# ScalarE's order of bank and weight cast in the FFN gate phases, turned round in both kinds of FFN

## The reference

```python
# first block, two layers; x (latent) and ctx (context) are 256 tokens each
def half_ffn(t, m, j):
    h = modulate(rmsnorm(t, norm_g[l, j]), m[3 * j], m[3 * j + 1])
    return t + 0.5 * m[3 * j + 2] * swiglu(h, ffn_w_gate[l, j // 2], ffn_w_up[l, j // 2], ffn_w_down[l, j // 2])
...
# second block, two layers; x only
x = x + 0.5 * swiglu_2(rmsnorm_2(x, ffn1_norm[l]), ffn1_w_in[l], ffn1_w_out[l])
...
x = x + 0.5 * swiglu_2(rmsnorm_2(x, ffn2_norm[l]), ffn2_w_in[l], ffn2_w_out[l])
```

## Time and profile before

| | |
|---|---|
| median of 3 runs | 3185.64 us (3184.75 to 3185.68) |
| the profiled execution's own time | 3185.47 us |
| its span, first to last instruction | 3183.7 us |
| PE busy | 3154.0 us, 99% |
| VectorE busy | 2373.9 us, 75% |
| ScalarE busy | 1346.6 us, 42% |
| GpSimd busy | 635.0 us, 20% |
| mean granted TensorE clock | 0.998 |

### The profile page before, as it was taken

One profiled execution on the slowest core, in us unless ns is written; L12 is line 12 of the kernel. 1 busy time (PEld: TensorE's weight loads), 2 busy tenths in 40 slices (PEclk: granted clock), 3 DMA queues, 4 the chain that ended last, 5 costly groups with the idle time before them and its releaser, 6 DMA issues.

```text
span 3183.7 us, 46362 instructions
## 1 busy us (share of the span) xinstructions
PE 3154.0 (99%) x17108; PEld 2708.8 (85%) x17108; DVE 2373.9 (75%) x3075; ACT 1346.6 (42%) x1987; POOL 635.0 (20%) x524
## 2 busy tenths in 40 slices
PE   9999999999999999999999999999999999999999
PEld 5888888888888888888888889889888889889988
DVE  4877957868787735566778887885888896885887
ACT  3222233212232224443546455565645546565643
POOL 2212322202321121001323230100222231100122
PEclk9999999999999999999999999999999999999999
DMA  6655514646365432334665665454665765453665
GB/s 235 209 156 175 162 57 147 201 139 188 96 198 176 139 102 87 106 106 140 195 187 163 196 177 169 133 152 140 184 193 174 201 186 172 127 157 114 192 193 151
DMA packets 771388, 507.47 MB, mean 159 GB/s; under 512 B 15108, under 2 KB 720720, under 8 KB 771216
## 3 DMA queue, kind: packets, MB, share of 16 engines
q1 hardware_dynamic: 770048, 503.51, 53.8%
q0 software_dynamic: 368, 1.38, 0.1%
q10 hardware_dynamic: 800, 0.24, 0.0%
HBM read 504.01 MB, written 1.05 MB: 159 GB/s over the span
## 4 chain that ended last, share of the span: by engine, by line
PE 51%; DVE 6%; issue 2%; ACT 2%; POOL 0%; DVEq 0%; ACTq 0%; POOLq 0%
PE bank L688 17%; PE bank L686 9%; PE bank L690 4%; PE bank L692 4%; PE bank L691 4%; PE bank L705 3%; PE bank L707 3%; PE bank L706 3%; PE bank L685 2%; DVE wlo_all L1675 2%; PE bank L1190 1%; ACT whi_all L1256 1%; PE bank L1016 0%; DVE xn_two L1773 0%; PE bank L1162 0%
## 5 line engine op out<-in xcount | busy, mean ns | idle before, releaser
L1675 DVE TENSOR_TENSOR wlo_all<-raw,whi_all 128x1024 fp32r<-128x1024 f32 (+3 forms) x768 | 1008.5, 1316 | 424.5 <-ACT whi_all L1256 421.8
L1256 ACT CAST whi_all<-raw 128x1024 fp32r<-128x1024 f32 (+3 forms) x768 | 833.6, 1091 | 1024.5 <-PE bank L692 551.4
L690 PE MATMUL bank<-xn_two,whi_all 128*128 128x512 f32 (+1 forms) x1616 | 587.9, 364 | 1.0 <-DVE xn_two L1849 1.0
L692 PE MATMUL bank<-xn_two,wlo_all 128*128 128x512 f32 (+1 forms) x1616 | 582.9, 361 | 0.0
L691 PE MATMUL bank<-xn_two,whi_all 128*128 128x512 f32 (+1 forms) x1616 | 582.7, 361 | 0.0
L688 PE MATMUL bank<-xn_two,whi_all 128*128 128x512 f32 x1540 | 550.4, 397 | 0.0
L2331 POOL CAST h_two<-silu_g 128x256 f32 (+1 forms) x176 | 209.3, 1189 | 1322.6 <-DVE silu_g L1914 753.4
L686 PE MATMUL bank<-xn_two,wlo_all 128*128 128x256 f32 x1760 | 456.1, 279 | 0.0
L686 PEld LDWEIGHTS bank<-xn_two,wlo_all 128*128 128x128 f32 x1760 | 332.5, 189 | 18.9
L690 PEld LDWEIGHTS bank<-xn_two,whi_all 128*128 128x128 f32 x1616 | 306.6, 190 | 47.5 <-DVE xn_two L1849 1.8
L691 PEld LDWEIGHTS bank<-xn_two,whi_all 128*128 128x128 f32 x1616 | 306.7, 190 | 45.7
(11 more groups left out here) (337 smaller groups left out, 4868.0 us busy)
## 6 DMA issues: line engine op xcount, KB each, us to landing
raw<-in_ffn_w_in SPq DMA_DIRECT2D x176, 512.0 KB, 3.8
raw<-in_w_in SPq DMA_DIRECT2D x168, 512.0 KB, 3.8
ada_w<-in_ada_w SPq DMA_DIRECT2D x128, 512.0 KB, 4.1
raw<-in_ffn_w_gate SPq DMA_DIRECT2D x88, 512.0 KB, 3.9
raw<-in_ffn_w_up SPq DMA_DIRECT2D x88, 512.0 KB, 4.2
raw<-in_ffn_w_down SPq DMA_DIRECT2D x32, 768.0 KB, 5.3
raw<-in_ret_w_in SPq DMA_DIRECT2D x48, 512.0 KB, 3.9
raw<-in_ffn_w_out SPq DMA_DIRECT2D x32, 768.0 KB, 4.9
```

The costliest lines, as they stand in the source:

```text
L690: pe.matmul(o, whi[s][:, k, :], hi, start=(k == 0), stop=False)
L692: return pe.matmul(o, wlo[s][:, k, :], hi, start=False, stop=(k == ks - 1))
L1256: act.copy(whi[s][:, 0:ks, :], raw[s][:, 0:ks, :]).then_inc(hi_done[s], 1)
L1675: tt(wlo[s][:, 0:ks, :], raw[s][:, 0:ks, :], whi[s][:, 0:ks, :].bitcast(F32), ALU.subtract).then_inc(lo_done[s], 1)
```

## The change

One expression in ScalarE's part of `do_ffn`:

```diff
-                    stream(f"{a['tag']}gu{half}", gate, weights_first=a["norm"]["late"])
+                    stream(f"{a['tag']}gu{half}", gate, weights_first=not a["norm"]["late"])
```

## The result

The changed kernel takes 3271.28 us (median of 4 runs, 3270.25 to 3272.57) against 3185.28 us: a ratio of 1.027, 95% interval 1.0257 to 1.0282. The forecast was 3284 us with a range of 3246 to 3308. The profiled execution has a span of 3269.7 us, 86.0 us over that of before.

What follows compares the result with a forecast made beforehand. PE bounds the kernel, VectorE only 0.33 us a pair quicker; the change makes VectorE the bound in late FFNs. 90.7 + 1.5 - 0.3 + 6.8 = 98.7 us over 3185.47 gives 3284 us, range 3246 to 3308.

Steps and rivals of the forecast that it cites:

- The pair: Late gate phases: VectorE's loop of two slots with ScalarE takes 6.76 us, against 5.26 before and PE's 5.59.
- R10: b01gu0, last round: start of VectorE's even reduce, counted from R0, the first; forecast at 2332.07.
- silu to split: Late gate phases: step of the pair with the cast in between, 1.39 us, taken from a11.
- The lead: Late gate phases: VectorE's lead is gone by pair 3 in gu0; PE waits from about pair 6 in gu1.
- L1885 term: b00gu0: eight L1885 in VectorE's queue, about 0.39 us each, four giving back 0.40 us each: +1.5 us.
- The multiply: Late FFNs: L1896's 0.83 us is half waiting on GpSimd and stays 0.83; were it free, the pair would be 6.36.
- Table loads: ScalarE: late gu0s lose 20, other FFNs gain 24, 1.28 us each; they cost nothing.
- The last product: Late dn phases: PE waits for GpSimd's last subtract, 2.6 us in dn0 and 3.2 us in dn1.
- The clock: Half-clock stretches after PE's eight waits for the last product: four taken, between 0 and 8, +6.8 us.
- The other four FFNs: a11's 0.29 us PE wait can go, wide FFNs' second table load is hidden: -0.3 us for all.
- No change: Rival: three slots of lead absorb the delay, decided by a pair at or below 5.59 us; 3185 us, chance 0.06.
- half clock for whole phases: Rival: clock falls for whole gate phases, a pair takes 11.2 us; 380 us more, 3566 us, chance 0.03.

Runs made afterwards that it cites:

- e3: e1, but in late FFNs VectorE splits the even slot behind the odd slot's product instead of ahead of its reduce; 3184.59 us (0.9998).
- e4: e1, but late FFNs leave out the multiply L1896, so the silu waits for the reduce; 3205.59 us (1.0065).
- e7: Changed kernel, but in late FFNs GpSimd's subtract (all but a phase's last) waits for VectorE's multiply L1896 of the next pair; 3246.15 us (1.0192).
- e2: Kernel before, but the other four FFNs (a00, a01, a10, a11) cast first, then bank; late FFNs as before; 3182.76 us (0.9995).
- e8: Changed kernel plus filler matmuls on PE between each late gu0 and its dn0 (eight asked, 16 in the trace); 3269.66 us (1.0268).
- e5: Changed kernel, but in late FFNs only gu0 takes the bank first, gu1 casts first as before; 3237.77 us (1.0165).
- e1: Kernel before, but only the four late FFNs take the bank first, then cast; the other four as before; 3273.52 us (1.0277).
- e6: Changed kernel, but in late FFNs only gu1 takes the bank first, gu0 casts first as before; 3216.68 us (1.0101).

## Why the prediction was right, and where it was off

**What bounds.** Right. PE had next to no wait to give back (1.2 us in the other four FFNs), VectorE had 0.33 us a pair to spare, and this is where the change struck.

**The pair.** Forecast 6.76, measured 6.78 and 6.85 in turn, every step within 0.07 us: the second kind has 1.50 instead of 1.43 us ahead of the split, as a11 before had 1.51 and 1.42. Of the 0.65 us by which b01gu0 exceeds the forecast, 0.5 us come so: the reduce R10 stands at 2332.58 where 2332.07 was forecast (2352.68 in the trace, less the 20.10). The rest is 0.07 us ahead of the last split, 0.02 us in it and 0.05 us from its end to dn0. e3 shows that the loss is VectorE's place behind the cast, and e4 and e7 that a step that gets shorter shortens the pair by as much. To take the price of "silu to split" from a11, which had the new order already, was what made the number exact.

**The lead.** Right: in b01gu0 PE starts pair 3 0.17 us late and waits from pair 4 on, in gu1 its first wait, 0.36 us, is at pair 6. The L1885 term was right too: b00gu0 shows 12.05 us since in the kernel before it held a half-clock stretch of 1.6 us (1711.4) that is no longer there; 13.65 less 12.1 is the 1.5 us forecast.

**The multiply.** Right, shown by e7. The rule that I cited from the Trainium skill (SBUF — State Buffer, "Who interferes with whom") agrees with e7's rows: 0.42 us where GpSimd's subtract starts behind the multiply, 0.83 us where it starts ahead.

**Table loads.** Right that they cost nothing here. The drain that the Trainium skill (ScalarE: Activation LUTs, "What ACT_TABLE_LOAD costs") adds to each switch shows in no row: in b01gu0 of the kernel before the cast ends at 2267.13, the load runs from 2267.15 to 2268.43 and the silu starts at 2268.44. e2 can't tell its size, since its 24 more loads lie in ScalarE's idle time; it shows that none of them is on the path, where 1.28 us each would be 31 us.

**The last product: the term that was mis-sized.** The forecast took the time from the last even reduce to GpSimd's last subtract as 7.19 us from the kernel before, and so a wait of 2.6 us in dn0. VectorE's rows of the changed kernel in b01gu0 (last even reduce, last product, splits):

```profile
2361.02 0.68 DVE L1894 TENSOR_REDUCE silu_g<-bank 128x256 f32<-128x512 f32 x1
...
2363.66 0.43 DVE L1910 TENSOR_TENSOR silu_g<-silu_g,square 128x256 f32<-128x256 f32 x1
2364.49 1.77 DVE L1675 TENSOR_TENSOR wlo_all<-raw,whi_all 128x1536 fp32r<-128x1536 f32 x1 [0.41 <-ACT whi_all L1256]
```

and GpSimd's last cast and subtract:

```profile
2364.26 0.40 POOL L2331 CAST h_two<-silu_g 128x256 f32 x1 [1.98 <-DVE silu_g L1910]
2364.84 2.03 POOL L2333 TENSOR_TENSOR h_two<-silu_g,h_two 128x256 f32 x1 [0.18 <-POOL h_two L2331]
```

It is 5.85 us (2361.02 to 2366.87). GpSimd's cast took 0.40 and not 1.75 us: VectorE's split came 0.41 us later, since ScalarE's cast was late, and so GpSimd's cast started 0.23 us ahead of the split and not behind it. It started ahead, by 0.02 to 0.24 us, in all eight dn phases of the changed kernel. e7 has a counter-example: in its b00dn0 the cast started behind the split (1791.68, the split at 1791.62) and took 1.95 us, and that dn0 lost 2.76 us where its other three lost 1.7. The forecast had seen the later split and put it down as a cost of 0.4 us; it was a gain of 1.35 us to GpSimd. By that, PE without a dip waits 1.25 us in dn0 and not 2.6, which is what e8 and e5 show (1.3). In dn1, PE waited twice:

```profile
2459.18 0.39 PE L686 MATMUL bank<-h_two,wlo_all 128*128 128x256 f32 x1 [0.99 <-POOL h_two L2333]
...
2463.49 0.39 PE L686 MATMUL bank<-h_two,wlo_all 128*128 128x256 f32 x1 [0.52 <-POOL h_two L2333]
```

0.99 us for the product of the last pair but one, which the forecast had not looked at, and 0.52 us for the last, 1.31 and 0.84 us by the weight loads. The first takes from the second and adds nothing. The size is off as in dn0: from the last even reduce to the end of the last subtract it is 5.56 us (2457.88 to 2463.44) where 6.65 was forecast, 1.1 us less, and dn1 lost 2.1 to 2.2 us and not 3.2.

**The clock: right that it falls, wrong to add it.** There were four dips, as forecast, and one fewer at the start of b00gu0. The number four is luck: it was taken as the middle of 0 to 8, and it came as four of four in dn0 and none in dn1. And the dips came in front of the wait for the last products and took its place: the forecast put 6.8 us for them on top of that wait. By these two errors together the dn phases cost 15.3 us and not 30.0. That is the 14.7 us by which those terms were over; for the gate phases the forecast was 3 us low (69.1, measured 72.2, and 73.8 with b00's missing dip put back), and with the other small terms it ends 13 us high.

**The other four FFNs.** Sign right, a gain of 1.2 us instead of 0.3: the forecast had looked for PE's waits in the gate phases only. Three of the four that went, 0.40 us in a11dn0 and 0.26 us each in a00dn1 and a01dn1, lie a few chunks into a dn phase, where PE comes to the gate phase's last products.

**The rivals.** No change, faster, and half clock for whole phases did not come. The point from which "no change" decides, a pair at or below 5.59 us, holds: e3 with 5.12 us loses nothing, e4 with 5.90 us loses 20 us.

**A better version.** None beats the kernel before by an amount that can be told. e2 is lowest, 2.4 us under, its interval holding 1.

## What to carry to other kernels

Where two in-order engines hand work to and fro, write down the loop of their steps and compare it with the bound engine's period; the busy shares (VectorE 75%, ScalarE 42%) say nothing of it. A wait costs what stands behind it in the queue, so an operand that will be late belongs behind other work that is ready, as in e3. And stalls in a row on one engine don't add: if PE is slowed ahead of a wait for a third party, that wait shrinks by as much.

## What of the hardware was not expected

GpSimd's 128x256 cast takes 0.40 us where VectorE is between instructions when it starts, even if VectorE's split follows 0.02 us later (dn1 phases of the changed kernel), 1.22 us where it starts behind a 128x1024 split and 1.75 us behind a 128x1536 one (the changed kernel's b01 has all of these): what looks like its usual 1.22 us is mostly a wait for VectorE.

The same wait of 1.95 us at the start of a late dn0 was followed by half clock in four of four places in the changed kernel, in four of four in e1 and in two of four in e5, with the same instructions; the 1.5 us wait there in e7 in none of four. The mixers' wait of 2.76 us came with half clock at its end in 16 of 20 places over the ten traces, and where it did not (one place in e6, two in e7, one in e8) PE had another wait, of 1.02 us, 4.5 us later. A stretch at 0.50 also stood at the start of b00gu0 in the kernel before, behind no wait of that size, and in none of the nine other traces. So whether a stall of some 2 us costs a dip can't be read from the program; what it cost here was 1.6 us where nothing hid it and 0.3 us in dn0, where a wait stood behind it.
